# Feed-forwards of two tiles that open tile by tile, and the order of the adaptive-norm sums

## The chip, the cores and the metric

The kernel runs on one core of a Trainium2 chip. The metric is the device time of one execution in microseconds; three runs of the kernel before gave 2516.59, 2522.62 and 2525.74 us, median 2522.62 us. The trace shown below is of one profiled execution that took 2516.55 us.

## The reference

Two stacked blocks are computed on 256 latent tokens and, in the second block, 256 context tokens as well; the model width is 1024 and all values are fp32.

```
def first_block(x, c, w_ada, ...):
    c_act = jax.nn.silu(c)
    for l in range(DEPTH):
        mod = c_act @ w_ada[l] + b_ada[l]
        sh_m, sc_m, gt_m, sh_f, sc_f, gt_f = jnp.split(mod[:, None, :], N_MOD, axis=-1)
        h = rms_norm(x, g_pre_mix[l]) * (1.0 + sc_m) + sh_m
        y = token_mixer(h, w_in[l], g_moba_out[l], g_dsa_out[l], w_out[l], cos, sin)
        x = x + gt_m * rms_norm(y, g_post_mix[l])
        h = rms_norm(x, g_pre_ffn[l]) * (1.0 + sc_f) + sh_f
        y = conv_glu_ffn(h, w_up_act[l], w_up_lin[l], w_conv[l], b_conv[l], w_down[l])
        x = x + gt_f * rms_norm(y, g_post_ffn[l])
    return x

def conv_glu_ffn(h, w_up_act, w_up_lin, w_conv, b_conv, w_down):
    a = causal_depthwise_conv(h @ w_up_act, w_conv, b_conv)
    return (jax.nn.gelu(a) * (h @ w_up_lin)) @ w_down
```

`token_mixer` is a projection, two attentions (one over selected blocks, one over keys ranked by an index) and an output product. `second_block` has per layer a gated feed-forward (`silu(h @ wg) * (h @ wu)) @ wd`), a convolution module (layer 0) or a windowed attention (layer 1), and a second gated feed-forward. Its layers take nine vectors each from `silu(c) @ mod_w[i] + mod_b[i]` and, for the context tokens, from `silu(c_ctx) @ mod_w[i] + mod_b[i]`. Only the last feed-forward works on the latent tokens alone.

## The kernel before

**Products.** A token tile is 128 tokens. Every fp32 product is made of three fp32r products of a high and a low part (lines L1141 to L1143). Weights come from HBM in units of 128x1024 fp32 (512 KB, issued on SyncE's queue, L1093, 8 buffers `raw`); ScalarE makes the high part `sh` (`upper`, L1399), VectorE the low part `sl` (`lower`, L1687). There are 6 slots of `sh` and `sl`: in `finish()` a unit gets its upper and its lower only when the unit six before it has been used by a product.

**Two forms of a product.** In `product()` the weights are stationary and the activations of two tiles stream (256 columns); the result lies with the output columns on the partitions, as the next product needs it. In `down()` the activations of one tile are stationary and 512 weight columns stream; the result lies with tokens on the partitions.

**The sums.** The adaptive-norm vectors are 384 sums of VectorE over a 128x1024 block of `w_ada` or `mod_w_2` (L1701, tile `mjunk`); those of `mod_w_2` run twice, for latent and context. They are strewn between other work: each step calls `pace()`, which adds the stage's number from `RATES` to a counter, places a sum for each whole one, and takes one action from the list `aside`. Where a vector is needed, `need()` places what is missing. After the last sum of `w_ada` (`(w_ada, 1, 47)`) the context is loaded (`ctx_load`, SyncE), and before the first of `mod_w_2` ScalarE makes the silu of the two condition vectors in `cB` (L1406).

**Stages.** Mixer of layer 0 (to about 200 us), feed-forward (200 to 386), mixer of layer 1 (395 to 553), feed-forward (553 to 757), then `ffn2(0,0)`, `conv`, `ffn2(0,1)`, `ffn2(1,0)`, windowed attention, and `ffn2(1,1)` from 2315 us on. Three feed-forwards work on two tiles: `ffn1` of both layers and `ffn2(1,1)`.

**How such a feed-forward opens.** The output product before it (`w_out`) runs tile by tile. `gate_half()` takes each half of a tile out of PSUM (gate1, L1786), adds it to `x` (gate2, L1796) and calls `norm_tile()`: sum of squares (ACT L1422), rsqrt (POOL), scaling (ACT L1439, DVE L1742, tile `PT`), 8 transposes on TensorE (`turn`, L1241), shift and scale on the way out of PSUM (ACT L1458, DVE L1760, tile `F`), and the split into `hH` (ACT L1476) and `hL` (DVE L1776). Tile 0 is turned while tile 1 still runs; then come `warm(14)` (28 products without a use, L1166), the turn of tile 1 (`finish_norms()`), `warm(5)` (10 more), and the products of all up columns, 128 columns (a chunk) of both up matrices at a time. A chunk of `ffn1` goes through glu1_a (ACT L1558, two DVE L1986), glu1_b (ACT L1566, DVE L1997) and glu1_c (ACT L1576, POOL).

**Gates.** A gate vector is sent from `gc` to HBM (`gsend`, L1060) and fetched back as rows on all partitions (`gfetch`, L1074, tile `G`), both on SyncE's queue.

Of the kernel before, what the change touches and what calls it, by code (L numbers as in the profile page):

```python
# [31 lines left out]
RATES = {"proj0": 0.8, "proj1": 0.65, "att": 0.0, "out": 0.0, "up0": 0.56, "down0": 0.6, "up1": 0.36, "down1": 0.5,  # L32
# [23 lines left out]
NCST = 384 + 32  # L56

# [17 lines left out]
class Plan:  # L75
# [98 lines left out]
    def rows(self, src, dst, gid, s):  # L174

        def fetch():
            self.add("gfetch", src=src, dst=dst, id=(gid, s), before=self.row_of.get(dst))
            self.row_of[dst] = (gid, s)
        return ([lambda: self.add("gsend", src=src)] if src else []) + [fetch]
# [29 lines left out]
    def norm_tile(self, hid, t, AB, s, st=None, wide=False, lag=0, early=False):  # L209
# [102 lines left out]
    def gate_half(self, t, half, b, gid, AB, hid, st2):  # L312
# [12 lines left out]
        self.rms_close(st2[t], 2)  # L325
        for j in range(2):
# [5 lines left out]
        self.norm_tile(hid, t, AB, 0, st, early=True)  # L332
# [65 lines left out]
    def mixer(self, l, hid, ab_next):  # L398
# [135 lines left out]
        for i in tiles:  # L534
            for half in range(2):
                for kp in (2, 3):
                    part(kp, half, taken[(kp, half)], [i], i == 1, banks[half][i] if kp == 3 else None)
                self.gate_half(i, half, banks[half][i], gid, AB, hid, st2)
# [20 lines left out]

    def ffn1(self, l, hid, ab_next):  # L560
# [9 lines left out]
        def middle(g):  # L570
            g["f"] = self.next("F", 3)
            self.add("glu1_b", **g)
            self.left(g["bu"])

        for c in range(KF):
# [3 lines left out]
            bu = self.product("w_up_lin", l, c * 128, slice(0, 256), ("h", hid))  # L579
            if late:  # L580
                late.pop(0)()
            g = dict(l=l, c=c, ba=ba, bu=bu, s=self.place("S", c % 2), fid=fid, u=self.u_at)
            self.add("glu1_a", **g)
            self.left(ba)
            late = [lambda g=g: middle(g), lambda g=g: self.add("glu1_c", **g)]
# [19 lines left out]
    def ffn2(self, l, half_i, tiles, hid, ab_next, cols=(slice(0, 256), slice(256, 512)), done2=None):  # L605
# [4 lines left out]
        else:  # L610
            self.warm(14)
            self.finish_norms()
            self.warm(5)
# [9 lines left out]
        for fh in range(2):  # L623
            fid = self.new()
            for c in range(HALF):
                cc = fh * HALF + c
                begun = bool(head)
                if head:
# [6 lines left out]
                g = dict(N=N, c=c, ba=ba, bu=bu, s=self.place("S", c % 2), f=self.next("F", 3), fid=fid, u=self.u_at)  # L635
# [1727 lines left out]
```

## Time and profile before

| what | us |
|---|---|
| three runs | 2516.59, 2522.62, 2525.74 |
| the profiled execution, its span | 2516.55, 2514.7 |
| TensorE busy | 2418.3 (96%) |
| VectorE busy | 1678.3 (67%) |
| ScalarE busy | 1079.9 (43%) |
| GpSimd busy | 390.8 (16%) |
| DMA, mean | 168 GB/s |

Busy times are sums over the span. The product records of TensorE overlap (the end of each is modelled), so the pace of products is read from start to start, and its idle time from the records in brackets. A row of a timeline that ends in `[2.79 <-DVE PT L1742]` says that the engine stood for 2.79 us before it and that VectorE's instruction at L1742 ended that.

### The profile page before, as it was taken

What the parts mean: (1) busy time and instruction counts of PE and PEld (TensorE: products, weight loads), DVE (VectorE), ACT (ScalarE), POOL (GpSimd) and SP (SyncE); (2) the same over time, 40 slices, a digit from 0 to 9 for tenths busy, and PEclk for the clock granted to TensorE, in tenths of its full rate; (3) what the DMA queues carried; (4) which work ended last, traced back from release to release, by engine and by line L of the source; (5) the groups of instructions that cost most, each with busy time, mean ns of one, the idle gap of its engine ahead of it and who ended that gap; (6) DMA issues with size and microseconds to landing.
All of it is one profiled execution on the core that took longest, in us unless ns stands there. A gap on an engine that the chain in (4) does not pass through costs nothing.

```text
span 2514.7 us, 34853 instructions
## 1 busy us (share of the span) xinstructions
PE 2418.3 (96%) x13166; PEld 2033.5 (81%) x13166; DVE 1678.3 (67%) x2618; ACT 1079.9 (43%) x1850; POOL 390.8 (16%) x431
## 2 busy tenths in 40 slices
PE   6899999989999999999979999999999999999998
PEld 5678988779979888887648888889888888777997
DVE  6957987858995776777865565566565566356554
ACT  4566545566554212236744322224322225344543
POOL 1101101111111101105850110100100110001101
PEclk9999999999999999999989999999999999999999
DMA  8765895647783554543212463442353444322662
GB/s 322 248 174 188 306 322 201 220 117 247 262 278 115 184 191 173 191 153 93 68 34 84 135 197 120 164 171 94 128 203 125 155 170 114 120 90 77 194 201 93
DMA packets 135880, 422.57 MB, mean 168 GB/s; under 512 B 28448, under 2 KB 32672, under 8 KB 135712
## 3 DMA queue, kind: packets, MB, share of 16 engines
q1 hardware_dynamic: 135152, 418.55, 49.7%
q8 instruction: 105, 1.72, 0.3%
q10 hardware_dynamic: 560, 1.79, 0.2%
q14 instruction: 63, 0.52, 0.1%
HBM read 419.17 MB, written 1.11 MB: 167 GB/s over the span
## 4 chain that ended last, share of the span: by engine, by line
PE 66%; DVE 2%; ACT 1%; POOL 1%; issue 0%; POOLq 0%; DVEq 0%; ACTq 0%
PE ps L1141 20%; PE ps L1142 20%; PE ps L1143 20%; PE ps L1336 2%; PE ps L1324 1%; POOL ap L2208 1%; PE ps L1241 1%; PE ps L1293 1%; PE ps L1304 1%; DVE ps L2033 0%; PE ps L1359 0%; PE ps L1348 0%; ACT F L1458 0%; DVE sl L1687 0%; DVE hL L1776 0%
## 5 line engine op out<-in xcount | busy, mean ns | idle before, releaser
L1399 ACT ACTIVATE sh<-raw 128x1024 fp32r<-128x1024 f32 x534 | 551.6, 1043 | 907.1 <-PE ps L1143 880.2
L1141 PE MATMUL ps<-hH,sh 128*128 128x256 f32 (+1 forms) x2560 | 839.3, 328 | 3.7 <-DVE hL L1776 2.7
L1142 PE MATMUL ps<-hL,sh 128*128 128x256 f32 (+1 forms) x2560 | 834.5, 326 | 0.0
L1143 PE MATMUL ps<-hH,sl 128*128 128x256 f32 (+1 forms) x2560 | 834.5, 326 | 0.0
L1687 DVE TENSOR_TENSOR sl<-raw,sh 128x1024 fp32r<-128x1024 f32 x534 | 639.7, 1218 | 102.2 <-ACT sh L1399 101.9
L1141 PEld LDWEIGHTS ps<-hH,sh 128*128 128x128 f32 x2560 | 481.5, 188 | 55.5 <-issue 8.0
L1142 PEld LDWEIGHTS ps<-hL,sh 128*128 128x128 f32 x2560 | 480.7, 188 | 49.2 <-issue 1.7
L1143 PEld LDWEIGHTS ps<-hH,sl 128*128 128x128 f32 x2560 | 481.3, 188 | 48.2
L1701 DVE CUSTOM_DVE_ANT_0 mjunk<-raw,cB,V 128x1024 bf16<-128x1024 f32 x384 | 499.2, 1300 | 28.4 <-DMA C<-in_cst 8.4
L2181 POOL TENSOR_TENSOR uLl<-F,uHh 128x256 fp32r<-128x256 f32 (+1 forms) x132 | 168.1, 1274 | 1175.7 <-ACT uHh L1576 1068.0
L1141 PE MATMUL ps<-sh,uHh 128*128 128x512 f32 x792 | 311.8, 394 | 2.5 <-DVE sl L1687 2.5
L1142 PE MATMUL ps<-sl,uHh 128*128 128x512 f32 x792 | 312.6, 395 | 0.0
L1143 PE MATMUL ps<-sh,uLl 128*128 128x512 f32 x792 | 312.5, 395 | 0.0
L2006 DVE TENSOR_TENSOR F<-S,ps 128x512 f32<-128x512 f32 (+1 forms) x88 | 54.7, 621 | 323.7 <-issue 302.1
L1141 PE MATMUL ps<-sh,hH 128*128 128x512 f32 (+2 forms) x480 | 192.4, 401 | 21.6 <-DVE hL L2070 7.3
L1143 PE MATMUL ps<-sh,hL 128*128 128x512 f32 (+2 forms) x480 | 186.3, 388 | 0.0
L1142 PE MATMUL ps<-sl,hH 128*128 128x512 f32 (+2 forms) x480 | 186.1, 388 | 0.0
L1141 PEld LDWEIGHTS ps<-sh,uHh 128*128 128x128 f32 x792 | 149.3, 189 | 36.9 <-DVE sl L1687 3.4
L1142 PEld LDWEIGHTS ps<-sl,uHh 128*128 128x128 f32 x792 | 149.4, 189 | 33.5
L1143 PEld LDWEIGHTS ps<-sh,uLl 128*128 128x128 f32 x792 | 149.5, 189 | 32.2
L1141 PEld LDWEIGHTS ps<-sh,hH 128*128 128x128 f32 x480 | 92.8, 193 | 43.8 <-issue 15.8
L2208 POOL TENSOR_TENSOR ap<-ap,FT 128x512 f32<-128x512 f32 x76 | 107.0, 1411 | 35.6 <-ACT FT L1618 26.2
(164 smaller groups left out, 2038.4 us busy)
## 6 DMA issues: line engine op xcount, KB each, us to landing
raw<-in_w SPq DMA_DIRECT2D x752, 512.0 KB, 4.7
G<-gates SPq DMA_DIRECT2D x14, 512.0 KB, 6.7
raw<-in_w SPq DMA_DIRECT2D x16, 256.0 KB, 4.5
cB<-in_rpb SPq DMA_DIRECT2D x64, 64.0 KB, 2.6
raw<-in_w SPq DMA_DIRECT2D x4, 492.0 KB, 5.9
S<-in_rows SPq DMA_DIRECT2D x6, 256.0 KB, 3.2
X<-in_x ACTq DMA_DIRECT2D x1, 1024.0 KB, 11.9
X<-in_ctx SPq DMA_DIRECT2D x1, 1024.0 KB, 6.0
```

The source lines that it names most:

```text
L1141: self.e.matmul(out, lh, rh, start=start, stop=False)
L1142: self.e.matmul(out, lh, rl, start=False, stop=False)
L1143: return self.e.matmul(out, ll, rh, start=False, stop=stop)
L1241: x = self.e.transpose(self.buf(p["b"])[:, k * 128:(k + 1) * 128], src[:, k * 128:(k + 1) * 128], ident)
L1293: x = self.e.matmul(ps[:, :], self.m["qT"][pr, c, i], self.m["kT"][pr, c, :], start=True, stop=True)
L1336: x = self.e.matmul(ps[:, :], wd[:, k, :], up[:, :, k:k + 256], start=k == 0, stop=k == n - 1)
L1399: self.e.activation(self.m["sh"][k % SPL][:, 0:w], self.m["raw"][r % RAW][:, 0:w], ACT.Copy).then_inc(self.sems["w_hi"], 1)
L1687: self.e.tensor_tensor(lo[:, 0:w], raw[:, 0:w], hi[:, 0:w].bitcast(F32), ALU.subtract).then_inc(self.sems["w_lo"], 1)
L1701: self.e.tensor_tensor_reduce(out=self.m["mjunk"][:, :], in0=raw[:, 0:D], in1=self.m["cB"][:, st, :], scale=1.0, scalar=o, op0=ALU.mult, o ...
L2006: self.e.tensor_tensor(F[:, 0:N], self.buf(s["s"])[:, 0:N], self.buf(s["bu"])[:, 0:N], ALU.mult).then_inc(self.sems["v_ps"], 1)
L2181: self.e.tensor_tensor(lo, self.buf(s["f"])[:, 0:N], hi.bitcast(F32), ALU.subtract).then_inc(self.sems["p_sb"], 1)
L2208: self.e.tensor_tensor(ap, ap, self.buf(f)[:, :], ALU.add).then_inc(self.sems["p_sb"], 1)
```

## The change

- **Order of the sums.** In the projection stage the rate holds only for the first blocks; for the others (`cb` 2 to 5, those beside the ranking and the attentions) it is `rank0` 0.3 and `rank1` 0.2. The second attention and `w_out` (`att`) go from 0 to 1.0. In all 384 sums stay. By stages: layer 0's projection and ranking have 13 sums before and 5 after from its third block on, the stage of the second attention and `w_out` 1 before and 9 after (one more falls just ahead of it), the feed-forward 34 and 32; in layer 1 the projection and ranking have 3 fewer, `w_out` 0 before and 9 after, and the feed-forward's up part 16 before and 13 after.
- **Opening tile by tile.** The three feed-forwards start with `by_tile()`: one shorter warm-up (`warm(7)`, `warm(14)` in `ffn2(1,1)`), then the first four chunks (512 columns) of both up matrices with `h` stationary, in 16 parts of 6 products of 512 columns. Tile 0's first six parts stand ahead of and behind the turn of tile 1. The results have tokens on the partitions: `utok` copies them to SBUF (ScalarE or VectorE), `uturn` turns them back with 16 transposes into two pairs of PSUM banks, and the chunks' activation chains run from those. In `ffn1` these four chains are issued beside the products of chunks 4 and 5, with no `pace()` between. The new `hold` and `ready` steps stop new uppers and lowers while tile 1 of `w_out` runs, so that the norm's instructions of both engines stand ahead of them; `second_parts()` (the split of tile 0's `h`) now stands ahead of tile 1's gate2.
- **Gates.** The vectors that become gates are laid so that a partition holds 8 neighbouring values, and a send writes 128 pieces of 32 bytes, where it wrote 1024 of 4 bytes. The fetch is put three actions behind the send.

The core of the diff (the new engine functions `utok` are plain copies of a bank to SBUF):

```
-RATES = {"proj0": 0.8, "proj1": 0.65, "att": 0.0, ...
+RATES = {"proj0": 0.8, "proj1": 0.65, "rank0": 0.3, "rank1": 0.2, "att": 1.0, ...
...
+        def send():
+            self.add("gsend", src=src)
+            while len(self.aside) < 3:
+                self.aside.append(lambda: None)
+            self.aside.insert(3, fetch)
+        return [send]
...
         if early:
             self.second_parts()
+        if held:
+            self.add("lowers")
+            self.add("ready", n=1)
...
         self.rms_close(st2[t], 2)
+        self.second_parts()
+        if held and t:
+            self.add("ready", n=1)
         for j in range(2):
...
+                self.rate = RATES[f"proj{l}"] if cb < 2 else RATES[f"rank{l}"]
...
+    def by_tile(self, names, hid, warm):
...
+        self.warm(warm)
+        self.add("hold", on=False)
+        one, two = ([take(n, j) for j in range(4)] for n in names)
+        A, B = [self.bank(), self.bank()], [self.bank(), self.bank()]
+        for j in range(3):
+            part(one[j], j, 0, A[0], False)
+        self.finish_norms()
+        part(one[3], 3, 0, A[0], False)
+        for j in range(2):
+            part(two[j], j, 0, B[0], False)
+        SA0 = stage(0, A[0], "a")
+        to = [self.bank(), self.bank()]
+        for j in range(4):
+            part(one[j], j, 1, A[1], True)
+            if j == 1:
+                turned(0, SA0, to)
+        for j in range(2):
+            part(two[j], j, 1, B[1], True)
...
     def ffn1(self, l, hid, ab_next):
         self.rate = RATES[f"up{l}"]
-        self.warm(14)
-        self.finish_norms()
-        self.warm(5)
-        self.aside += [lambda: None] * 8
+        to, up, rest = self.by_tile((("w_up_act", l), ("w_up_lin", l)), hid, 7)
+        self.aside += [lambda: None] * 5
...
+        for c in range(4, KF):
             ba = self.product("w_up_act", l, c * 128, slice(0, 256), ("h", hid))
-            if late:
+            if c == 4:
+                rest()
+            if c in (4, 5):
+                while late:
+                    late.pop(0)()
+                begin(2 * c - 8, to[c - 4], up[c - 4], 0)
+            late.pop(0)()
+            bu = self.product("w_up_lin", l, c * 128, slice(0, 256), ("h", hid))
+            late.pop(0)()
+            if c in (4, 5):
+                begin(2 * c - 7, to[c - 4], up[c - 4], 256)
                 late.pop(0)()
...
+            begin(c, ba, bu, 0)
             self.pace(2)
...
-        dst = bass.AP(tensor=self.dram["gates"].tensor, offset=k * D, ap=[[1, P], [P, 8], [1, 1]])
+        dst = bass.AP(tensor=self.dram["gates"].tensor, offset=k * D, ap=[[8, P], [1, 8]])
```

**VectorE at an opening.** The next two pieces are VectorE's rows from tile 1's first gate1 of `w_out` in layer 0 on (after: gate1 is L1919, the shift and scale L1893, the split L1909, gate2 L1929, the scaling L1875, `lower` L1820). Before:

```order
L1786 TENSOR_TENSOR S<-ps,G 128x512
L1687 TENSOR_TENSOR sl<-raw,sh 128x1024
L1786 TENSOR_TENSOR F<-ps,G 128x512
L1760 TENSOR_SCALAR F<-ps,A,V 128x128 x4
L1796 SCALAR_TENSOR_TENSOR X<-S,st,X 128x512
L1796 SCALAR_TENSOR_TENSOR X<-F,st,X 128x512
L1776 TENSOR_TENSOR hL<-F,hH 128x4x128 x2
L1742 TENSOR_SCALAR PT<-X,st 128x512
L1760 TENSOR_SCALAR F<-ps,A,V 128x128 x4
L1776 TENSOR_TENSOR hL<-F,hH 128x4x128 x2
L1687 TENSOR_TENSOR sl<-raw,sh 128x1024 x3
```

After:

```order
L1919 TENSOR_TENSOR S<-ps,G 128x512
L1919 TENSOR_TENSOR F<-ps,G 128x512
L1893 TENSOR_SCALAR F<-ps,A,V 128x128 x4
L1909 TENSOR_TENSOR hL<-F,hH 128x4x128 x2
L1929 SCALAR_TENSOR_TENSOR X<-S,st,X 128x512
L1929 SCALAR_TENSOR_TENSOR X<-F,st,X 128x512
L1820 TENSOR_TENSOR sl<-raw,sh 128x1024
L1875 TENSOR_SCALAR PT<-X,st 128x512
L1820 TENSOR_TENSOR sl<-raw,sh 128x1024 x3
L1893 TENSOR_SCALAR F<-ps,A,V 128x128 x4
L1909 TENSOR_TENSOR hL<-F,hH 128x4x128 x2
```

The split of tile 0's `h` (`hL<-F,hH`) has moved ahead of tile 1's two gate2, and the lower that stood between the two gate1 has moved behind them.

**VectorE around the context vectors.** The next two pieces are of the feed-forward of layer 1 (`ISA mjunk` is a sum, L1986 and L1997 are the activation chain; after: L1834, L2127 and L2138). Before, from the sum `(w_ada, 1, 47)` on; the row that follows the last one is the first sum that reads the context's `cB`:

```order
L1701 ISA mjunk,V<-raw,cB,V 128x1024
L1701 ISA V 128x1
L1687 TENSOR_TENSOR sl<-raw,sh 128x1024
L1997 TENSOR_TENSOR F<-S,ps 128x256
L1687 TENSOR_TENSOR sl<-raw,sh 128x1024
L1986 SCALAR_TENSOR_TENSOR S<-ps,V,S 128x255
L1986 SCALAR_TENSOR_TENSOR S<-ps,V,S 128x254
L1687 TENSOR_TENSOR sl<-raw,sh 128x1024
L1997 TENSOR_TENSOR F<-S,ps 128x256
L1687 TENSOR_TENSOR sl<-raw,sh 128x1024
L1986 SCALAR_TENSOR_TENSOR S<-ps,V,S 128x255
L1986 SCALAR_TENSOR_TENSOR S<-ps,V,S 128x254
```

After; the first `ISA mjunk` is `(w_ada, 1, 47)`, the last row the first sum that reads the context's `cB`:

```order
L2127 SCALAR_TENSOR_TENSOR S<-ps,V,S 128x255
L2127 SCALAR_TENSOR_TENSOR S<-ps,V,S 128x254
L2138 TENSOR_TENSOR F<-S,ps 128x256
L2127 SCALAR_TENSOR_TENSOR S<-ps,V,S 128x255
L2127 SCALAR_TENSOR_TENSOR S<-ps,V,S 128x254
L1834 ISA mjunk,V<-raw,cB,V 128x1024
L1834 ISA V 128x1
L1820 TENSOR_TENSOR sl<-raw,sh 128x1024 x2
L2138 TENSOR_TENSOR F<-S,ps 128x256
L2127 SCALAR_TENSOR_TENSOR S<-ps,V,S 128x255
L2127 SCALAR_TENSOR_TENSOR S<-ps,V,S 128x254
L1834 ISA mjunk,V<-raw,cB,V 128x1024
```

Before, two chunks' lowers (four) and chains stand between the two sums; after, two lowers and one chunk's chain, and ahead of the first sum the chains of five chunks follow each other with single lowers between.

**VectorE at the end of layer 1's mixer.** From the lowers ahead of the last tile's softmax divisor (`rd`, of the second attention) to the first gate1 of `w_out`. Before:

```order
L1687 TENSOR_TENSOR sl<-raw,sh 128x1024 x2
L1776 TENSOR_TENSOR hL<-F,hH 128x4x128
L1967 RECIPROCAL rd<-den 128x8
L1970 TENSOR_TENSOR O<-ps,rd 128x512
L1977 TENSOR_SCALAR O<-O,st 128x512
L1711 SCALAR_TENSOR_TENSOR A<-V 128x8
L1687 TENSOR_TENSOR sl<-raw,sh 128x1024 x2
L1786 TENSOR_TENSOR S<-ps,G 128x512
```

After, the same place:

```order
L1820 TENSOR_TENSOR sl<-raw,sh 128x1024
L1909 TENSOR_TENSOR hL<-F,hH 128x4x128
L1834 ISA mjunk,V<-raw,cB,V 128x1024
L1834 ISA V 128x1
L2100 RECIPROCAL rd<-den 128x8
L2103 TENSOR_TENSOR O<-ps,rd 128x512
L2110 TENSOR_SCALAR O<-O,st 128x512
L1834 ISA mjunk,V<-raw,cB,V 128x1024
L1834 ISA V 128x1
L1844 SCALAR_TENSOR_TENSOR A<-V 128x8
L1820 TENSOR_TENSOR sl<-raw,sh 128x1024
L1919 TENSOR_TENSOR S<-ps,G 128x512
```

Two sums stand among these rows that did not before, one ahead of the divisor and one behind the last scaling (`O<-O,st`); two of the four lowers have moved away.

## Rows read from the trace of the kernel before

**Rows 1.** TensorE's waits: line, releaser: us in total, times, longest

```profile
PE ps L1141 <- DVE sl L1687: 5.6, 4, 2.2
```

**Rows 2.** Stretches: length; busy of PE, PEld, DVE, ACT, POOL; PEclk; DMA share; GB/s

```profile
92.00:125.00 33.00, 27.16 (x135) 20.56 (x134) 32.10 (x84) 18.07 (x42) 1.38 (x3) 0.93 0.64 217
160.00:187.00 27.00, 24.95 (x148) 20.37 (x148) 11.42 (x32) 17.31 (x50) 0.79 (x2) 0.94 0.72 148
214.00:228.00 14.00, 14.00 (x124) 14.00 (x125) 12.04 (x17) 8.04 (x12) 0.74 (x1) 1.00 0.64 226
430.00:482.00 52.00, 47.30 (x242) 36.50 (x241) 50.30 (x134) 28.03 (x56) 4.32 (x9) 1.00 0.64 226
601.00:748.00 147.00, 143.68 (x1019) 132.75 (x1017) 141.54 (x209) 84.58 (x133) 25.30 (x26) 1.00 0.76 263
```

**Rows 3.** Timeline, 159 to 195 us: start, us, engine, line, operation, tiles, [idle before]

```profile
159.51 0.71 PE L1287 MATMUL ps<-qkT 64*128 64x128 f32 x4 [2.06 <-DVE mst L1940]
...
194.38 0.50 PE L1141 MATMUL ps<-sh,hH 128*128 128x512 f32 x1 [1.45 <-DVE hL L1776]
```

**Rows 4.** Timeline, first opening (layer 0, 200 to 214 us)

```profile
200.53 1.99 ACT L1399 ACTIVATE sh<-raw 128x1024 fp32r<-128x1024 f32 x2
...
200.86 6.21 PE L1166 MATMUL ps<-C 128*128 128x256 f32 x28
...
203.00 1.50 ACT L1458 ACTIVATE F<-ps,V,A 128x128 f32<-128x128 f32 x4
...
208.02 1.29 DVE L1776 TENSOR_TENSOR hL<-F,hH 128x512 fp32r<-128x512 f32 x2 [1.53 <-ACT hH L1476]
...
209.86 1.06 PE L1241 MATMUL ps<-C,PT 128*128 128x128 f32 x8 [2.79 <-DVE PT L1742]
...
213.92 0.36 PE L1141 MATMUL ps<-hH,sh 128*128 128x256 f32 x1 [0.84 <-DVE hL L1776]
```

**Rows 5.** Timeline, second opening (layer 1)

```profile
553.99 6.21 PE L1166 MATMUL ps<-C 128*128 128x256 f32 x28
...
568.82 0.36 PE L1141 MATMUL ps<-hH,sh 128*128 128x256 f32 x1
```

**Rows 6.** Timeline, third opening (last feed-forward)

```profile
2315.87 6.21 PE L1166 MATMUL ps<-C 128*128 128x256 f32 x28
...
2326.87 0.35 PE L1141 MATMUL ps<-hH,sh 128*128 128x256 f32 x1 [0.84 <-DVE hL L1776]
```

**Rows 7.** Timeline, two neighbouring products of 512 columns

```profile
744.87 0.40 PE L1142 MATMUL ps<-sl,uHh 128*128 128x512 f32 x1
745.10 0.39 PE L1143 MATMUL ps<-sh,uLl 128*128 128x512 f32 x1
```

**Rows 8.** Timeline, one chunk's activation chain in layer 1

```profile
584.05 0.55 ACT L1558 ACTIVATE S<-ps,V 128x256 f32<-128x256 f32 x1
...
584.63 1.00 DVE L1986 SCALAR_TENSOR_TENSOR S<-ps,V,S 128x255 f32<-128x255 f32 x2 [0.63 <-ACT S L1558]
...
586.47 0.40 ACT L1566 ACTIVATE S<-S 128x256 f32<-128x256 f32 x1
...
587.88 0.42 DVE L1997 TENSOR_TENSOR F<-S,ps 128x256 f32<-128x256 f32 x1
```

**Rows 9.** Timeline, VectorE around the context vectors

```profile
585.55 1.27 DVE L1701 CUSTOM_DVE_ANT_0 mjunk<-raw,cB,V 128x1024 bf16<-128x1024 f32 x1
...
586.75 1.22 DVE L1687 TENSOR_TENSOR sl<-raw,sh 128x1024 fp32r<-128x1024 f32 x1
...
601.26 1.28 DVE L1701 CUSTOM_DVE_ANT_0 mjunk<-raw,cB,V 128x1024 bf16<-128x1024 f32 x1 [4.75 <-ACT cB L1406]
...
603.80 1.22 DVE L1687 TENSOR_TENSOR sl<-raw,sh 128x1024 fp32r<-128x1024 f32 x1
...
614.83 1.22 DVE L1687 TENSOR_TENSOR sl<-raw,sh 128x1024 fp32r<-128x1024 f32 x1
```

**Rows 10.** SyncE's waits

```profile
SPq L1074 <- DMA gates<-gc: 91.4, 13, 12.1
```

More of the change, by code:

```diff
@@ L537, in mixer @@
                     part(kp, half, taken[(kp, half)], [i], i == 1, banks[half][i] if kp == 3 else None)
-                self.gate_half(i, half, banks[half][i], gid, AB, hid, st2)
+                    if i and not half and kp == 2:
+                        self.add("hold", on=True)
+                self.gate_half(i, half, banks[half][i], gid, AB, hid, st2, True)
                 if i == 0 and half == 0:
@@ L558, in index_scores, with part, stage, turned @@
         self.aside[0:0] = steps
+    def by_tile(self, names, hid, warm):
+        take = lambda n, j: self.unit(True, [n + (k, 0, 512) for k in (2 * j, 2 * j + 1)])
+        def part(n, j, t, b, last):
+            self.add("down", unit=n, ks=[2 * j, 2 * j + 1], tiles=[(t, (t, b))], last=last, full=b if j == 3 else None,
+                     act=("h", hid), nk=KD)
+        def stage(t, b, on):
+            S = self.place("S", 2 + t)
+            self.add("utok", b=b, S=S, on=on)
+            self.left(b)
+            return S
+        def turned(t, S, to):
+            self.add("uturn", S=S, t=t, to=to)
+        self.warm(warm)
[16 more added lines that the diff above has]
+            part(two[j], j, 1, B[1], True)
+        SA1 = stage(1, A[1], "v")
+        for j in range(2, 4):
+            part(two[j], j, 0, B[0], False)
+        turned(1, SA1, to)
+        SB0 = stage(0, B[0], "a")
+        for j in range(2, 4):
+            part(two[j], j, 1, B[1], True)
+        up = [self.bank(), self.bank()]
+        turned(0, SB0, up)
+        SB1 = stage(1, B[1], "v")
+        return to, up, lambda: turned(1, SB1, up)
     def ffn1(self, l, hid, ab_next):
         self.rate = RATES[f"up{l}"]
-        self.warm(14)
-        self.finish_norms()
-        self.warm(5)
-        self.aside += [lambda: None] * 8
+        to, up, rest = self.by_tile((("w_up_act", l), ("w_up_lin", l)), hid, 7)
+        self.aside += [lambda: None] * 5
         gid = self.gates_later("w_ada", l, 5, ("g_post_ffn", (l,)), 1)
@@ L627, in ffn2 @@
                 begun = bool(head)
+                if len(tiles) == 2 and cc < 4:
+                    ba, bu, o = to[c // 2], up[c // 2], 256 * (c % 2)
+                    if c == 0:
+                        rest()
+                    g = dict(N=N, c=c, ba=ba, bu=bu, o=o, s=self.place("S", c % 2), f=self.next("F", 3), fid=fid, u=self.u_at)
+                    if late:
+                        late.pop(0)()
+                    self.add("glu2_a", **g)
+                    if c % 2:
+                        self.left(ba, bu)
+                    late.append(lambda g=g: self.add("glu2_b", **g))
+                    continue
                 if head:
@@ L900, in finish @@
         out, n, ctx, top, used, order, lower, loads = [], 0, False, 0, set(), [], [], []
+        held, more = False, 0
         for s in self.steps:
             real = "unit" in s and s["kind"] != "place"
+            if s["kind"] == "hold":
+                held, more = s["on"], 0
+                continue
+            if s["kind"] == "ready":
+                more += s["n"]
+            if s["kind"] == "lowers":
+                out += lower
+                lower = []
+                continue
             if real:
@@ L911, in finish @@
                         break
+                    if split and held and not (real and n <= s["unit"]):
+                        if not more:
+                            break
+                        more -= 1
                     if split:
@@ L1169, in warm, with uturn @@
         self.done("mm", ("left", s["b"]))
+    def uturn(self, s):
+        t, S = s["t"], self.buf(s["S"])
+        if t == 0:
+            for b in s["to"]:
+                self.wait_ge(self.gone(b))
+        self.wait_ge(self.got("tok", s["S"]))
+        for c in range(4):
+            o = 256 * (c % 2) + 128 * t
+            x = self.e.transpose(self.buf(s["to"][c // 2])[:, o:o + 128], S[:, c * 128:(c + 1) * 128],
+                                 self.m["C"][:, C_ID:C_ID + 128])
+        x.then_inc(self.sems["tr"], 1)
+        self.done("tr", ("left", s["S"]), *([("full", b) for b in s["to"]] if t else []))
     def proj(self, s):
```

87 lines of the change are left out of this document (55 added, 32 removed).

## The prediction

> **What bounds the kernel now.** I read the page first, then the list of TensorE's waits, the stretches, and the timelines of the three places that the change touches. TensorE is the engine that sets the time almost everywhere; it waits for finished weights only 5.6 us in all, four times, 2.2 us at the longest [rows 1]. In most stages, then, only work taken off TensorE or idle time taken out of it counts. There are three exceptions, and each is a place of the change. In the ranking of layer 0 VectorE is busy 32.10 of 33 us and TensorE 27.16; in the same place of layer 1 it is 50.30 of 52 against 47.30 [rows 2]: there VectorE sets the pace. At the three openings TensorE does nothing of use for 13.06 us (200.86 to 213.92), 14.83 us (553.99 to 568.82) and 11.0 us (2315.87 to 2326.87) [rows 4 to 6]. And in the feed-forward of layer 1 VectorE is busy 141.54 of 147 us, TensorE 143.68 [rows 2]: both are nearly full, so whatever makes VectorE late there stays late.
>
> **The change part by part.** All differences are against the profiled execution of 2516.55 us; the median of the runs, 2522.62, lies 6.07 above it, and I add that at the end.
>
> One sum costs VectorE 1.20 us (585.55 to the next start at 586.75, [rows 9]).
>
> (a) Ranking of layer 0. Eight sums go. Five of them stand in the full stretch: 5 x 1.20 = 6.0 us, about all that TensorE stands idle there (33 - 27.16 = 5.84). The other three stand where VectorE has room; of the wait of 2.06 us at 159.51 [rows 3], which is behind one of them, I credit 1.2. Together -7.2. Bounds: -2.1 (only that wait goes, since the ranking's own work is in the way) and -9.6 (all eight).
>
> (b) Ranking of layer 1. Three sums fewer, 3 x 1.20: -3.6. Bounds: 0, and -4.7, the idle time of TensorE (52 - 47.30).
>
> (c) The 18 sums that now stand in the second attentions and `w_out`. From 160 to 187 us VectorE is busy 11.42 of 27 [rows 2], so nine sums (10.8 us) find room. But the order is fixed: in each layer one stands ahead of the last divisor and one behind the last scaling, and what follows them is the chain to the last `hL`, for which TensorE already waited 1.45 us at 194.38 [rows 3]. The first is on the path (1.20), of the second I count 0.8: 2.0 per layer, +4. Bounds: 0, and 18 x 1.20 = +21.6. I stay near the lower end, since the room is measured.
>
> (d) First opening. ScalarE's two uppers (1.99 us at 200.53) no longer stand ahead of the turned tile's shift, so that starts at 201.0 where it was 203.00, takes 1.50, and the split follows: ScalarE's half and then VectorE's, some 1.9 us, ready at about 204.4, where it ended at 209.3 [rows 4]. A part is six products at 0.23 us [rows 7], 1.39 us; six parts of tile 0 are 8.3 us, done by 212.7. Tile 1 is later than before by the 1.29 us of the split, which now stands ahead of its gate2: 215.2 in place of 213.92. By then 8.3 us of products are done where before 1.3 were, so -7.0 (a product of 512 columns costs as much as two of 256, 14.00 us / 124 = 0.113 each [rows 2], so that nothing is gained or lost by the form). Two times eight transposes come in; eight take about 0.87 (0.109 each, from the 1.06 us of eight less the drain), +1.75. Then the chains: six of them are issued beside chunks 4 and 5, whose products take 2 x 48 x 0.113 = 10.9 us. One chain is 0.55 + 1.00 + 0.40 + 0.42 [rows 8], another 0.40 for the last ScalarE step, and four handoffs of some 0.06: 3.0 us, and they run one behind the other, 18 us. ScalarE and VectorE fall 7 us back; the uppers and lowers are up to six units, three chunks, ahead, and hide most of it. I take +2.5 (bounds 0 and +7.1). Together -2.7, bounds -5.3 and +1.9.
>
> (e) Second opening. The same 7.0, and the 1.77 us by which this opening was longer goes too: -8.7, with the transposes -7.0. What is late next is the context. The sums of `mod_w_2` wait for `cB`, which is loaded only after the sum (w_ada, 1, 47): that sum ended at 586.8, and VectorE stood 4.75 us and went on at 601.26, 14.5 us later [rows 9]. TensorE did not wait: by the order the lowers up to chunk 6 were done. After the change the sum stands behind the chains of chunks 0 to 3, 4 and half of 5. They begin when the first product of chunk 4 is done, at 568.82 - 7.0 + 4.5 x 5.42 = 586.2 (a chunk is 48 x 0.113 = 5.42); 5.6 chains x 3.0 + 1.2 put the sum's end at 604.2, and VectorE goes on at 618.7. Two context sums (2.5) and two lowers (2.4) later, at 623.6, the second unit of chunk 9 is ready; before it was at 616.0 (614.83 + 1.2, [rows 9]). By the order TensorE has lowers through chunk 8, 568.82 - 7.0 + 9 x 5.42 = 610.6; chunk 9's first is ready at 622.4, so it stands for about 11 us. VectorE then has nothing to spare to the end of the stage, so its lateness, 7.6 us, stays. Two more sums are left behind this point (2.4), and a gate's fetch that held up loads comes later; I let these cancel and take +7 for the whole stage, its opening included. Bounds: -7 (no stall) and +11 (three lowers between the chains, 3.6, also in full).
>
> (f) Third opening. Its warm-up stays 28 products long (6.21 us, to 2322.1) and tile 0 is ready about then; products begin at about 2322.6 in place of 2326.87, -4.2, plus 1.75 for transposes and 0.8 for the copies they wait for: -1.7, bounds -4 and +1.
>
> (g) Gates. SyncE waited 91.4 us for the gates to come back, 13 times [rows 10], but behind these fetches are weight loads for which TensorE hardly waits: 0.
>
> Sum: -7.2 - 3.6 + 4 - 2.7 + 7 - 1.7 = -4.2, 2512.3 on the profiled execution's scale, 2518.4 on the median's.
>
> **The rivals.** First, the context costs nothing in layer 1: the chains overlap (ScalarE takes one chunk while VectorE has another), the sum ends by 593, and VectorE is back by 608, before TensorE's work ends at 610.6. For it: the wait before the change cost TensorE nothing. Against it: each chain's first step is issued behind the last step of the one before. (e) is then -7: sum -18.2, 2504.
>
> Second, the sums in the second attention are all on the path. For it: TensorE waits at 194.38 for VectorE already, and a sum of 1.28 us cannot be put off once begun. Against it: VectorE is busy less than half of that stage. It decides from 12 sums on the path: with all 18, (c) is +21.6 and the sum +13.4, 2536, slower.
>
> Third, the clock. From 92 to 125 us TensorE waited often, and the granted clock was 0.93 on the mean, so (1 - 0.93) x 33 = 2.3 us went there [rows 2]. The shorter warm-ups and the new wait of 11 us could each bring such a fall: four of them, +9.2, sum +5, 2528. Against it: the products start earlier, too, so the idle time ahead of them is shorter. The Trainium skill, "TensorE: Matmul & The Clock Gate", Part 1, says that the array falls back to half rate when idle and that activity releases it; the trace agrees in that its fall is where TensorE waited.
>
> Fourth, the ranking does not give its sums back: (a) and (b) at their upper bounds, -2.1 and 0. The sum is +4.5, 2527.
>
> **How the numbers follow.** The forecast gets 0.50, the first rival 0.24, the second 0.11, the third 0.07, the fourth 0.08. About 0.5% (12.6 us) is what a measurement of this kernel can tell from no change. Below 2510.0 lie the first rival nearly whole and the low tail of the forecast: 0.31. Above 2535.2 lie most of the second and the tails of the last two: 0.11. The rest is 0.58. The forecast's own range is 2508 to 2528; to leave out no more than 2 in 10 it has to reach over most of the first rival and up to the second: 2498 to 2534.
>
> **What would show it.** Right: no sum more than needed from 92 to 125 us and TensorE's share there up by about 6 us; first products some 9 us earlier at the first two openings; a wait of TensorE of about 11 us for a lower near 605 to 620 us, behind a VectorE wait for `cB`; two sums on the way to the last `hL` of each `w_out`. Wrong: no such wait for `cB`'s sake, or TensorE waiting over 10 us more in the second attentions than before.

## The result, and the profile after

The changed kernel takes 2531.28 us (median of 6 runs, 2528.67 to 2532.72), the kernel before 2520.16 (6 runs, 2516.59 to 2525.74): ratio 1.0047, 95% interval 1.0031 to 1.0062. It is slower by about 11 us, where the prediction had 4 us less; the time lies inside the range given. The profiled execution took 2530.3 us.

The page of the changed kernel, its first lines: engine, busy us, share of the span, instructions.

```profile
span 2528.5 us, 34241 instructions
PE 2420.4 (96%) x12868; PEld 2021.3 (80%) x12868; DVE 1685.0 (67%) x2624; ACT 1086.6 (43%) x1856; POOL 393.0 (16%) x431
```

Busy times are as before within 0.7%; most of the time is lost in waits. TensorE's list of waits and SyncE's, as in [rows 1] and [rows 10]:

```profile
PE ps L1253 <- DVE sl L1820: 22.2, 14, 8.1
```

```profile
SPq L1186 <- DMA gates<-gc: 2.1, 1, 2.1
```

TensorE's waits for lowers went from 5.6 to 22.2 us, and SyncE's for gates from 91.4 to 2.1. The stages, from one warm-up's first row to the next one's (worked out from those starts in the two traces; the last column is the end of the span less the start of the convolution's warm-up):

| kernel | start to 2nd warm-up | mixer 0 | feed-forward 0 | mixer 1 | feed-forward 1, ffn2(0,0), part of conv | rest |
|---|---|---|---|---|---|---|
| before | 47.5 | 153.4 | 194.1 | 159.0 | 727.6 | 1233.2 |
| changed | 47.5 | 146.4 | 201.3 | 161.7 | 742.5 | 1229.1 |
| difference | 0 | -7.0 | +7.2 | +2.7 | +14.9 | -4.1 |
| predicted | 0 | -5.2 | -2.7 | -1.6 | +7 | -1.7 |

The first opening itself came out nearly as worked out. Its timeline, to be held against [rows 4]:

```profile
193.91 3.19 PE L1278 MATMUL ps<-C 128*128 128x256 f32 x14
...
197.59 0.47 PE L1253 MATMUL ps<-sh,hH 128*128 128x512 f32 x1 [0.50 <-DVE hL L1909]
...
208.62 0.47 PE L1253 MATMUL ps<-sh,hH 128*128 128x512 f32 x1 [0.90 <-DVE hL L1909]
```

The first product comes 3.7 us after the warm-up's start, where it came 13.06 us after; the first product of tile 1 comes 14.7 us after it (14.3 worked out), behind a wait of 0.90 us.

The two rankings, against the same stretches in [rows 2]:

```profile
92.00:125.00 33.00, 31.93 (x174) 24.43 (x173) 31.77 (x87) 19.64 (x46) 3.42 (x4) 1.00 0.59 191
430.00:482.00 52.00, 49.11 (x244) 37.98 (x243) 46.81 (x127) 28.00 (x56) 5.82 (x8) 0.97 0.62 207
```

TensorE gained 4.8 us in the first (about 6 predicted) and 1.8 in the second (3.6).

The context in layer 1, as in [rows 9] (VectorE, then ScalarE, then TensorE):

```profile
619.28 1.28 DVE L1834 CUSTOM_DVE_ANT_0 mjunk<-raw,cB,V 128x1024 bf16<-128x1024 f32 x1 [7.96 <-ACT cB L1531]
```

```profile
617.24 1.91 ACT L1531 ACTIVATE cB<-cB 128x2048 f32<-128x2048 f32 x1 [4.70 <-DMA cB<-in_cc]
```

```profile
623.18 0.55 PE L1253 MATMUL ps<-hH,sh 128*128 128x256 f32 x1 [8.06 <-DVE sl L1820]
```

That is the wait of about 11 us that the prediction put near 605 to 620 us; it is 8.06 and ends at 623.18. What the prediction did not name is in the next piece, VectorE in the middle of the same feed-forward:

```profile
681.95 2.36 DVE L1820 TENSOR_TENSOR sl<-raw,sh 128x1024 fp32r<-128x1024 f32 x2
684.22 0.41 DVE L2138 TENSOR_TENSOR F<-S,ps 128x256 f32<-128x256 f32 x1
685.57 1.00 DVE L2127 SCALAR_TENSOR_TENSOR S<-ps,V,S 128x255 f32<-128x255 f32 x2 [0.94 <-ACT S L1691]
686.49 1.27 DVE L1834 CUSTOM_DVE_ANT_0 mjunk<-raw,cB,V 128x1024 bf16<-128x1024 f32 x1
```

Both lowers of the chunk stand together ahead of `F`. ScalarE needs `F` for glu1_c, and its next instruction is the first step of the following chain, which VectorE needs at once: 0.94 us in which a full engine stands. Over this stage that is the largest group of VectorE's waits:

```profile
DVE S L2127 <- ACT S L1691: 14.2, 16, 0.9
```

Why the lowers pair up is in `finish()`. `ready` sets `upto` to the number of all units, and `top` is a maximum that never comes down. Before, a sum let no upper run ahead; after the first `ready` every sum does, so that two uppers come between two products and both lowers are put ahead of the next one. The diff in the section on the change does not show these lines (e2's edit below does), and its text gives `hold` and `ready` only as a stop of uppers and lowers; VectorE's order shows the effect as `sl<-raw,sh 128x1024 x2` (the piece shown above around the context has one).

### The profile page after: what moved, and what is told of

Same layout as the page of the kernel before. It is cut to its first block, busy times and chain, and to the rows that moved or that the text cites. A ratio compares the mean times of both kernels' runs of the same rounds, so it can differ in the third digit from the quotient of the medians.

```text
span 2528.5 us, 34241 instructions
## 1 busy us (share of the span) xinstructions
PE 2420.4 (96%) x12868; PEld 2021.3 (80%) x12868; DVE 1685.0 (67%) x2624; ACT 1086.6 (43%) x1856; POOL 393.0 (16%) x431
## 4 chain that ended last, share of the span: by engine, by line
PE 66%; DVE 2%; ACT 1%; POOL 1%; issue 0%; POOLq 0%; DVEq 0%; ACTq 0%
PE ps L1253 20%; PE ps L1254 20%; PE ps L1255 20%; PE ps L1461 2%; PE ps L1449 1%; POOL ap L2349 1%; PE ps L1366 1%; PE ps L1418 1%; PE ps L1429 1%; DVE ps L2174 0%; PE ps L1484 0%; PE ps L1473 0%; PE ps L1278 0%; DVE ps L2196 0%; DVE sl L1820 0%
## 5 line engine op out<-in xcount | busy, mean ns | idle before, releaser
L1253 PE MATMUL ps<-hH,sh 128*128 128x256 f32 (+1 forms) x2368 | 790.3, 334 | 19.4 <-DVE sl L1820 18.2
L1254 PE MATMUL ps<-hL,sh 128*128 128x256 f32 (+1 forms) x2368 | 783.6, 331 | 0.0
L1255 PE MATMUL ps<-hH,sl 128*128 128x256 f32 (+1 forms) x2368 | 783.5, 331 | 0.0
L1820 DVE TENSOR_TENSOR sl<-raw,sh 128x1024 fp32r<-128x1024 f32 x534 | 639.9, 1225 | 122.8 <-ACT sh L1524 122.0
L1834 DVE CUSTOM_DVE_ANT_0 mjunk<-raw,cB,V 128x1024 bf16<-128x1024 f32 x384 | 498.0, 1297 | 36.4 <-DMA C<-in_cst 8.6
L1253 PEld LDWEIGHTS ps<-hH,sh 128*128 128x128 f32 x2368 | 446.6, 189 | 72.6 <-issue 24.9
L1255 PEld LDWEIGHTS ps<-hH,sl 128*128 128x128 f32 x2368 | 446.7, 189 | 48.2
L1254 PEld LDWEIGHTS ps<-hL,sh 128*128 128x128 f32 x2368 | 445.5, 188 | 49.3 <-issue 1.7
L1253 PE MATMUL ps<-sh,hH 128*128 128x512 f32 (+2 forms) x576 | 230.8, 401 | 21.8 <-DVE hL L1909 12.7
L1254 PE MATMUL ps<-sl,hH 128*128 128x512 f32 (+2 forms) x576 | 222.5, 386 | 0.0
L1255 PE MATMUL ps<-sh,hL 128*128 128x512 f32 (+2 forms) x576 | 222.2, 386 | 0.0
L1253 PEld LDWEIGHTS ps<-sh,hH 128*128 128x128 f32 x576 | 110.5, 192 | 49.7 <-issue 21.1
L1255 PEld LDWEIGHTS ps<-sh,hL 128*128 128x128 f32 x576 | 110.3, 191 | 22.4
```

The costliest lines, as they stand in the source:

```text
L1253: self.e.matmul(out, lh, rh, start=start, stop=False)
L1254: self.e.matmul(out, lh, rl, start=False, stop=False)
L1255: return self.e.matmul(out, ll, rh, start=False, stop=stop)
L1820: self.e.tensor_tensor(lo[:, 0:w], raw[:, 0:w], hi[:, 0:w].bitcast(F32), ALU.subtract).then_inc(self.sems["w_lo"], 1)
L1834: self.e.tensor_tensor_reduce(out=self.m["mjunk"][:, :], in0=raw[:, 0:D], in1=self.m["cB"][:, st, :], scale=1.0, scalar=o, op0=ALU.mult, o ...
```

## The experiments

Each run has its median and its ratio to the kernel before, measured on the same chip; stage times are of the one profiled execution. `e1`, `e5` and `e11` are edits of the kernel before, `e2`, `e3`, `e4` and `e6` of the changed kernel, `e7` is e2 and e4 together, `e8` and `e14` build on e2, and `e9`, `e10`, `e12`, `e13` on e7.

**e1: the sums alone.**

```
-RATES = {... "proj1": 0.65, "att": 0.0, ...     (kernel before)
+RATES = {... "proj1": 0.65, "rank0": 0.3, "rank1": 0.2, "att": 1.0, ...
+                self.rate = RATES[f"proj{l}"] if cb < 2 else RATES[f"rank{l}"]
```

> The kernel before with the new rates of the sums alone (rank0 0.3, rank1 0.2, att 1.0), openings and gates as before. The trace of the changed kernel starts the first opening 6.95 us earlier than before and the second one 2.9 us later than before, with a feed-forward of layer 0 between them that loses 7.1. If the order of the sums alone makes the 6.95, the opening here starts near 193.9 us too, and the kernel is 5 to 8 us faster than before unless layer 1's mixer gives it back. Theory A (sums on the second attention's chain cost little): layer 1's mixer is within 1 us of before, total -7. Rival B (the order of the sums is what costs layer 1's mixer 2.7 us): the mixer of layer 1 takes 2 to 3 us more here as well, total -4.

2516.60 us, ratio 0.9984 (0.9967 to 1.0). Mixer 0 took 150.0 us (-3.4, not -7), mixer 1 160.7 (+1.7): nearer to B. Half of the gain in mixer 0 is not the sums' alone (see (a) and (c) further down). Layer 0's feed-forward, which this edit does not touch, took 198.9 in place of 194.1 without any new wait; see the end. Layer 1's, with what follows, took 721.2 (-6.4).

**e2: the bound.**

```
-                if s["kind"] == "ready":
-                    s["upto"] = len(self.units)
-                top = max(top, s["upto"] if "upto" in s else s["unit"] + 1)
-                while n < (len(self.units) if real else min(top, len(self.units))):
+                if s["kind"] != "ready":
+                    top = max(top, s["upto"] if "upto" in s else s["unit"] + 1)
+                while n < (len(self.units) if real or s["kind"] == "ready" else min(top, len(self.units))):
```

> The changed kernel, but a ready step no longer raises for good the bound to which uppers may run ahead at a sum; this changes only where the lowers stand. In the changed kernel, from the first opening on, every sum brings both lowers of a chunk ahead of the chain's product with the second matrix, and VectorE then stands 0.94 us per chunk for ScalarE (16 times, 14.2 us in the feed-forward of layer 1; before, 7.2 us). Theory P (these pairs make the two feed-forwards' waits for lowers): the 16 waits go, layer 1's feed-forward gains 6 to 8 us and layer 0's 4 to 6, total about 2519. Theory Q (VectorE is short of time because it stands idle in the openings and for the context): under 3 us of gain, 2528 to 2532, since the gaps only move.

2509.71 us, 0.9964 (0.9951 to 0.9978): 21.6 less than the changed kernel, and faster than before. Feed-forward 0 takes 190.1 us (-11.2), feed-forward 1 with what follows 732.1 (-10.4). VectorE in the same place, and its waits in feed-forward 1:

```profile
662.98 1.22 DVE L1819 TENSOR_TENSOR sl<-raw,sh 128x1024 fp32r<-128x1024 f32 x1
664.12 0.41 DVE L2137 TENSOR_TENSOR F<-S,ps 128x256 f32<-128x256 f32 x1
664.45 1.22 DVE L1819 TENSOR_TENSOR sl<-raw,sh 128x1024 fp32r<-128x1024 f32 x1
665.58 0.99 DVE L2126 SCALAR_TENSOR_TENSOR S<-ps,V,S 128x255 f32<-128x255 f32 x2
```

```profile
DVE S L2126 <- ACT S L1690: 3.0, 4, 0.9
```

The second lower now fills the 0.94 us. 14.2 - 3.0 = 11.2 us of VectorE's waits go, and the stage gains 10.4: theory P, at nearly twice the size expected; in layer 1 the 7.2 us of before were not a floor. TensorE's waits for lowers in layer 0's feed-forward, the changed kernel and then e2:

```profile
PE ps L1253 <- DVE sl L1820: 6.6, 5, 2.7
```

```profile
PE ps L1252 <- DVE sl L1819: 0.2, 1, 0.2
```

That is 6.4 of the 11.2 us there. About 2 more are another thing: half of the changed kernel's up products run there at a slower pace, which nearly none of e2's do (see the end).

**e3: sums in the opening.**

```
+            if j < sums:            (behind each part of tile 1, six in all, layer 0)
+                self.fill(1)
-"up0": 0.56
+"up0": 0.44
```

> The changed kernel with six sums placed behind parts of tile 1 in the opening of layer 0's feed-forward, and the rate behind it lowered (0.56 to 0.44), so that the stage has 22 sums as before. VectorE is busy 20.5 of 30.1 us in that opening, so six sums (7.2 us) find room. Theory Q (idle time of VectorE in the opening comes back as waits for lowers): the waits at 247 to 345 us (8 us with the small ones) shrink by 5 to 8 us, total 2524 to 2526. Theory P (pairs of lowers): with 16 sums in place of 22 in the chunks a quarter of the pairs go, 1 to 2.5 us, total 2529.

2529.77 us, 1.0042 (1.0023 to 1.0062): within the changed kernel's spread. Feed-forward 0 gained 4.7 us, nearly Q's size, and mixer 1 3.1, but the stage of layer 1's feed-forward, where nothing was edited, took 4.5 more (747.0). As a cause of the whole loss Q falls; what VectorE's idle time in the opening is worth by itself this run leaves open.

**e4: the context early.**

```
+            while self.jobs and self.jobs[0][:2] == ("w_ada", 1) and names[0] == ("w_up_act", 1):
+                self.fill(1)        (behind the first part of tile 1 in layer 1's opening)
```

> The changed kernel with the last sum of w_ada moved into layer 1's opening, so that the context vectors are loaded there. VectorE then no longer stands 7.96 us for them and TensorE no longer 8.2 us at 623 us. If the late context is a cost by itself, it goes in full: -8 to -12, total 2519 to 2523. Rival (VectorE is full to the end of the stage whatever happens there, so only VectorE's own idle time counts): the gain is VectorE's 8 us, of which some is lost as chunks 4 to 6 still carry six chains: -4 to -6, total 2525 to 2527. No gain would mean that the wait stood beside another one.

2527.53 us, -3.8 of the changed kernel; the stage went from 742.5 to 736.7 in the profiled execution, which is the slowest of ten. The rival's size: behind the wait, the paired lowers kept VectorE full.

**e5: pairs in the kernel before.**

```
+                if real and self.kinds[s["unit"]][1] and self.units[s["unit"]][1][0][0] == "w_up_act":
+                    top = len(self.units)        (kernel before, one change)
```

> The kernel before, changed in one thing only: from layer 0's up products on, uppers may run ahead at a sum, as in the changed kernel, so that wherever a sum stands between two chunks both lowers of a chunk stand together ahead of the chain's product. If the pairs alone make VectorE stand for ScalarE (theory P), this kernel loses with openings as before: 0.94 us per chunk with a sum, 5 to 10 us in each layer's feed-forward where VectorE is full, total 2526 to 2538, and the waits of L1988 for ScalarE's first step show it. Rival (pairs cost only behind the serial chains of the new opening): within 3 us of before, 2518 to 2523.

2535.11 us, 1.0066 (1.0044 to 1.0088). The old openings with the pairs are 15.8 us slower than without; feed-forward 0 takes 201.6 us, as in the changed kernel, feed-forward 1 with what follows 737.8. VectorE's waits in layer 1, 7.2 us before (7 times):

```profile
DVE S L1988 <- ACT S L1560: 18.0, 18, 1.7
```

So the raised bound by itself costs more than the whole change did. In layer 1 the way is the one of theory P: with VectorE's waits, TensorE's for lowers rise from 3.4 to 6.4 us. In layer 0 the trace does not show it. VectorE stands 21.1 us for ScalarE there (8.9 before), but TensorE waits for no lower at all; its products run at the slower of two paces, which alone is 4.7 of the 7.4 us:

```profile
230.00:330.00 100.00, 100.00 (x851) 100.00 (x851) 81.19 (x122) 54.58 (x84) 12.55 (x17) 1.00 0.82 275
```

e1 has the same 851 products in this stretch without any pairs. So in layer 0 the pairs are shown to make TensorE wait only together with the new opening; whether they have a part in the pace is open.

**e6: early uppers, split lowers.**

```
-                out += lower
-                lower = []
+                k = 1 if s["kind"] == "prod" and self.units[s["unit"]][1][0][0] in ("w_up_act", "w_up_lin") else len(lower)
+                out += lower[:k]
+                lower = lower[k:]
```

> The changed kernel, with uppers as early as there (the bound stays raised), but one lower ahead of each product of the up matrices, so that the second one of a pair stands behind the chain's product again. If the uncovered handoff to ScalarE is the cost, it goes nearly whole: 2509 to 2515, and the 14.2 us of VectorE's waits for ScalarE's first step in layer 1 fall under 5. If it is the earlier uppers on ScalarE that cost (they stand ahead of a chain step there), little changes: 2526 to 2531.

2510.82 us, 0.9965 (0.9953 to 0.9977), the same as e2, with 3.0 us of those waits:

```profile
DVE S L2128 <- ACT S L1692: 3.0, 4, 0.9
```

It is the uncovered handoff, not ScalarE's earlier uppers in the feed-forwards.

**e7: e2 with e4's edit.**

> The bound lowered again (2509.7 us) and the last sum of w_ada moved into layer 1's opening. TensorE's wait of 8.4 us near 611 us is the largest left in the feed-forwards. If it is the context's and stands alone, it goes: -6 to -9, total 2501 to 2504. Rival (the serial chains of chunks 0 to 5 make VectorE late by themselves): half of it stays, 2505 to 2508.

2500.13 us, 0.9925 (0.9906 to 0.9945): -9.6 against e2, 724.2 in place of 732.1 in that stage. Without the pairs the late context is worth its full wait.

**e8: the old opening in layers 0 and 1.** e2, with `warm(14)`, `finish_norms()`, `warm(5)` and all chunks in order in `ffn1`.

> The bound lowered again, and the feed-forwards of both first layers open as before (two warm-ups, no part of tile 0 ahead of tile 1); the last feed-forward opens tile by tile, and the order of the sums, the hold of uppers and the gates are the changed kernel's. It says what the opening tile by tile is worth in layers 0 and 1. By the prediction's terms without the pairs it loses about 4 us in layer 0 and gains about 5 to 8 in layer 1, where the late context goes: 2506 to 2510. Rival (each opening is worth the 5 to 7 us of idle time that it takes out): 2519 to 2522.

2498.74 us, 0.9926 (0.9900 to 0.9951), faster than expected and 11 less than e2. Feed-forward 0 takes 193.5 us (3.4 more than e2), feed-forward 1 with what follows 724.7 (7.4 less, no late context), mixer 1 154.8 (4.8 less). Of the last, 1.3 us lie between the stage's two warm-ups, a stretch that takes 13.0 to 13.2 us in eight of the 16 traces and 14.4 or 14.5 in the others, whatever the edit; 2.4 lie between there and TensorE's wait of 1.94 us for `hL` ahead of the last divisor. Only 1.1 lie behind that wait, where one sum less stands (two waits of TensorE, 1.20 and 1.33 us in the trace of e2, are gone).

So the opening tile by tile, the largest part of the change, gains 3.4 us in layer 0 and loses 7.4 in layer 1 (e2 against e8), or nothing there with the context early (e7). What e8 keeps of the change, the order of the sums, the new gates, the hold and the last feed-forward's opening, makes the whole 20.6 us by which it is faster than the kernel before; the sums alone make 3.8 (e1) and the gates alone 4.1 (e11).

**e9: one sum less on the chain.** e7 with `"att": 0.85`.

> e7_bound_context with one more change: the rate of the sums in the second attention is 0.85 in place of 1.0, so that layer 1's w_out has 8 sums in place of 9 and the one behind the last scaling goes. In e2_bound TensorE waits there for the last scaling (1.35 us of excess) and for the last hL (1.50); in e8_bound_old_opening, which has 8 sums there, both waits are absent. Theory (a sum on that chain is paid in full, beyond its 1.20 us): layer 1's mixer takes 2.5 to 5 us less, total 2495 to 2498. Rival (the waits only move to the next step of the chain): 2499 to 2501.

2499.58 us (2494.95 to 2505.52), 0.9912 (0.9893 to 0.9931). Mixer 1 takes 157.2 us, 2.3 less than e7, but not by the theory. The sum behind the last scaling still stands there in the trace (530.15 us), TensorE still waits 1.15 us for the last `hL`, and from the wait ahead of the last divisor to the next warm-up it takes 15.4 us in both; an earlier sum has gone. The theory is not tested by this run. The medians differ by 0.6 us only, and no gain can be told from them.

**e10: the old gates.** e7 with `gsend`, the fetch and the layout as before.

> e7_bound_context with the gates as before: 1024 pieces of 4 bytes, fetched at the next action. SyncE then waits some 90 us behind the fetches again (2.1 us in the changed kernel). Theory (weights come early enough, the gates are worth nothing): 2499 to 2502. Rival (raw loads held up behind the fetch cost where VectorE is full, as at 641 us before, where VectorE stood 2.93 us): 2 to 4 us slower, 2502 to 2505.

2517.68 us, 0.9988 (0.9976 to 1.0): 17.5 us more than e7 (15.9 by the two ratios, as they ran on two chips), far outside both. Mixer 0 takes 151.7 us (+5.3), feed-forward 0 198.4 (+8.3), mixer 1 163.6 (+4.1), in a profiled execution that is 5 us above the median. SyncE and ScalarE in the second attention of layer 0:

```profile
158.32 0.43 SPq L1164 DMA_DIRECT2D gates<-gc  x1
159.77 1.09 SPq L1197 DMA_DIRECT2D raw<-in_w  x2
172.59 0.33 SPq L1178 DMA_DIRECT2D G<-gates  x1
172.97 3.34 SPq L1197 DMA_DIRECT2D raw<-in_w  x6
```

```profile
173.42 1.06 ACT L1516 ACTIVATE sh<-raw 128x1024 fp32r<-128x1024 f32 x1 [2.20 <-DMA raw<-in_w]
174.38 0.56 ACT L1668 COPY PT<-ps 128x512 f32<-128x512 f32 x1
179.39 1.06 ACT L1516 ACTIVATE sh<-raw 128x1024 fp32r<-128x1024 f32 x1 [4.44 <-DMA raw<-in_w]
180.35 0.57 ACT L1668 COPY PT<-ps 128x512 f32<-128x512 f32 x1
```

The fetch stands 14.3 us behind the send, six raw blocks behind the fetch, an upper waits for one of them, and the attention's `PT`, for which TensorE waits (4.42 us at 180.97), is queued behind that upper on ScalarE.

**e11: the new gates alone** (kernel before).

> The kernel before with the new gates alone (128 pieces of 32 bytes, fetched three actions later). e10_old_gates lost 17.5 us by the old gates: SyncE stood from 158.8 to 172.6 us and from 520.1 to 533.6 us behind a fetch, in the second attentions, where the raw blocks of the new sums were queued behind it, and TensorE then waited 4.6 and 5.9 us for ScalarE's PT there. Theory (the old gates cost only where loads behind them are due soon; before has no sums in the second attentions): -1 to -5 us against before, 2515 to 2519. Rival (SyncE's 90 us of waits cost wherever they stand): -10 to -17, 2503 to 2510.

2516.83 us, 0.9982 (0.9969 to 0.9996), -4.1: the theory. Alone the gates are worth a quarter of what they are worth beside the moved sums.

**e12: new layout, fetch at once.** e7 with `return [send, fetch]`.

> e7_bound_context with the new layout of the gates, but the fetch at the next action as before. If the layout is what frees the queue (a send of 128 pieces lands much sooner than one of 1024), most of the 17.5 us stays won: 2500 to 2505. If the three actions in between are what frees it, the stalls come back: 2510 to 2518.

2499.62 us, 0.9926 (0.9907 to 0.9944), as e7. The same place as in e10:

```profile
159.98 0.43 SPq L1171 DMA_DIRECT2D gates<-gc  x1
161.43 1.08 SPq L1203 DMA_DIRECT2D raw<-in_w  x2
166.49 0.33 SPq L1184 DMA_DIRECT2D G<-gates  x1
```

The fetch goes out 6.5 us after the send, where it was 14.3.

**e13: old layout, fetch later.** e7 with `gsend` and `lanes` as before.

> e7_bound_context with the old layout (1024 pieces of 4 bytes), but the fetch three actions later. The counterpart of e12_fetch_at_once: if the actions in between are enough, 2500 to 2505; if the send takes longer than they do or disturbs loads, 2508 to 2518.

2512.14 us, 0.997 (0.9958 to 0.9981): 12 us of the 17.5 stay lost. The layout is what counts, and the three actions are not long enough for the old send: SyncE still waits 25.1 us for gates, in e12 15.9.

**e14: the parts together.** Layer 0 and the last feed-forward tile by tile, layer 1 as before, `"att": 0.85`.

> The best parts together: the bound lowered, layer 0's and the last feed-forward open tile by tile, layer 1's opens as before, the sums of the second attention at 0.85 so that layer 1's w_out has 8 as in e8_bound_old_opening. Layer 0's feed-forward took 190.1 us in e7_bound_context and 193.5 in e8_bound_old_opening; if the parts add up, this is 3.4 us faster than e8: 2493 to 2497. Rival (sums that leave layer 0 load layer 1, which is full): 2498 to 2502.

2499.89 us, 0.9923 (0.9904 to 0.9941): the rival. Feed-forward 0 is 2.7 us shorter than in e8, mixer 1 1.1 longer; in the median nothing is left. e7, e8, e9, e12 and e14 all lie at 2499 to 2500, 0.7 to 0.9% faster than before.

## Why the prediction was wrong

- **(a) was right, and (c) with the new gates.** The mark is the product that stood at 159.51 in [rows 3]; here it is in the changed kernel and in e1:

```profile
150.53 0.71 PE L1412 MATMUL ps<-qkT 64*128 64x128 f32 x4 [0.50 <-DVE mst L2073]
```

```profile
151.78 0.71 PE L1288 MATMUL ps<-qkT 64*128 64x128 f32 x4 [0.51 <-DVE mst L1941]
```

  Counted from the warm-up with which the stage starts in the table, it comes after 112.1 us before and after 103.1 in both of these: -9.0 for (a)'s -7.2, by the sums alone. From it to the next warm-up the changed kernel takes 2.0 us more, as (c) has it. With the old gates (e1) it takes 5.6 more, with a wait of 3.56 us for the attention's `PT`: the moved sums were not cheap there without the new gates.
- **(b) and (c), mixer 1: -1.6 predicted, +2.7 measured.** The same product in layer 1, before, changed and in e2:

```profile
513.90 0.71 PE L1287 MATMUL ps<-qkT 64*128 64x128 f32 x4 [0.85 <-DVE mst L1940]
```

```profile
515.59 0.71 PE L1412 MATMUL ps<-qkT 64*128 64x128 f32 x4 [1.63 <-DVE mst L2073]
```

```profile
501.85 0.71 PE L1411 MATMUL ps<-qkT 64*128 64x128 f32 x4 [0.50 <-DVE mst L2072]
```

  It comes 105.7, 105.9 and 101.7 us after the stage's second warm-up: once the bound is undone the three sums give back 4.0 us, where (b) has 3.6, and the raised bound takes it away (e6, which keeps the bound, is at 105.7). Behind it (c)'s +2 is +1.2, and +3.3 in e2. The other 1.3 us lie between the warm-ups (see e8).
- **(d): the opening is right, a term beside it was left out.** -2.7 was worked out; against the old opening, both without the pairs, it is -3.4 (e2 against e8), and first products came 9.4 us sooner after the warm-up. The step that failed is "The uppers and lowers are up to six units, three chunks, ahead, and hide most of it": it takes the place of the lowers as given and puts VectorE's wait for ScalarE behind a pair of them at nothing. With the pairs undone the stage is at -4.0 (e2), with them at +7.2; of the 11.2 us between, 6.4 are TensorE's waits for lowers and about 2 the pace.
- **(e): +7 predicted, +14.9 measured.** VectorE's sum ended at 606.7 (604.2 worked out), the context's sums began at 619.28 (618.7), TensorE stood 8.06 us (11). The sentence that failed is the last one, that the rest cancels: VectorE stood 11.2 us more in handoffs behind the pairs, and the stage is 10.4 us longer with them (e2). Without the pairs it is at +4.5 against the kernel before and at +7.4 against the old opening (e8), near the prediction.
- **(f): -1.7 predicted, -1.5 measured** from the last warm-up to the end (198.9 to 197.4 us). The other 2.6 us of the last column lie ahead of it and are not explained.
- **(g): 0 predicted, -17.5 measured** in the kernel without the pairs and with the context early (e10 against e7). "TensorE hardly waits" for the loads behind a fetch held for the kernel before (-4.1, e11). It did not hold after the sums had moved into the stretch behind the fetch. Here the Trainium skill would have warned: "DMA: Bandwidth & Descriptors", Specifications, puts the least transfer for line rate at 512 bytes. Both layouts lie far under it (4 and 32 bytes); the runs show that between them 1024 pieces or 128 still make 14.3 or 6.5 us.
- **The rivals.** The first (no late context) did not happen; e7 shows that it would have been worth 9.6 us. The second's place was wrong: the changed kernel is slower, but its second attentions and `w_out` took only 2.0 and 1.2 us more. The third: the clock did fall at the new wait, to its lower level from 619.5 to 626.4 us (0.50 granted), but the granted clock of the whole run is 0.988 in both profiled executions, so it decided nothing. The fourth did not happen in layer 0 (-9.0); in layer 1 it did (+0.2), by the raised bound.

The pairs were in the order of instructions that stood beside the prediction (`sl<-raw,sh 128x1024 x2`). They were counted as two lowers of 1.20 us; what had stood between them was not asked for. That handoff, put at nothing, is what turned the sign: without the pairs the changed kernel is some 10 us faster than before (e2), with them 11 us slower. That the time still fell inside the range is luck, since the range was drawn for other causes.

## What to carry to other kernels

On an engine that is full, look at what stands between two instructions that hand work to another engine and back: an independent instruction there is cover, and moving it costs the handoff each time (0.94 us, some 12 times a stage) although no busy time changes. A new bound that only ever rises changes the order of everything behind it, so compare the order far behind the edit too. And when work is moved into a stretch, look up which queue it loads from and what blocks that queue there: a wait that cost nothing may then be on the path.

## What the runs showed that was not expected

Products of 256 columns run at one of two paces, 113 or 118 ns from start to start, for stretches of tens of us, and the same kernel part can take either. The same 100 us of layer 0's up products, before and e1, both with no wait of TensorE:

```profile
230.00:330.00 100.00, 100.00 (x885) 100.00 (x884) 90.15 (x136) 59.05 (x92) 16.11 (x19) 1.00 0.89 307
```

```profile
230.00:330.00 100.00, 100.00 (x851) 100.00 (x850) 86.63 (x130) 56.86 (x90) 14.58 (x18) 1.00 0.85 294
```

885 products against 851 at the same granted clock: 4%, 4.7 us on that feed-forward (198.9 against 194.1). e5 has the slower pace there, too, and the changed kernel has it for half of these products. The pace is seen to change at a wait or where another group of products begins; what sets it was not tried. A difference of under 5 us between stages of two traces is therefore weak evidence by itself, that of e2 and e8 in layer 0 as well, though both have the faster pace there.
